# Attention results: added by VectorE one pair of steps later and stored by the loading queue

## The reference, cut to what matters

```
z      = q @ k.T * scale
log_nb = where(key < query, log_sigmoid(-z), 0)
excl   = reverse_cumsum(log_nb) - log_nb
a      = where(key < query, exp(z + log_sigmoid(-z) + excl), 0)
out    = a @ v
```

## Time and profile before

| quantity | value |
|---|---|
| median of 3 runs (lowest, highest) | 4323.52 us (4323.11, 4325.3) |
| time of the profiled execution | 4328.02 us |
| span inside that execution | 4326.2 us |
| TensorE, VectorE, ScalarE busy share of the span | 95%, 63%, 58% |
| attention, from about 1030 to 2330 us | about 1300 us |

### The profile page before, as it was taken

One profiled execution on the slowest core, in us unless ns is written; L12 is line 12 of the kernel. 1 busy time (PEld: TensorE's weight loads), 2 busy tenths in 40 slices (PEclk: granted clock), 3 DMA queues, 4 the chain that ended last, 5 costly groups with the idle time before them and its releaser, 6 DMA issues. The chain is left out here.

```text
span 4326.2 us, 83388 instructions
## 1 busy us (share of the span) xinstructions
PE 4105.9 (95%) x27983; PEld 3104.5 (72%) x27985; DVE 2704.5 (63%) x3882; ACT 2488.0 (58%) x3370; POOL 598.0 (14%) x790
## 2 busy tenths in 40 slices
PE   8999989997999999999998999869999999999997
PEld 6888867774555555555555888758888888888886
DVE  3222235668888888888885555467666655555665
ACT  4222225556887887888885333246665655545665
POOL 0000002231000000000000111102332332323332
PEclk9999999998999999999999999989999999999999
DMA  5444353313112112111103434247666654555674
GB/s 200 182 144 180 146 180 110 124 68 115 31 31 61 31 31 61 31 31 53 36 7 104 147 145 155 106 167 258 226 241 221 227 202 165 204 193 199 242 262 144
DMA packets 308634, 590.36 MB, mean 136 GB/s; under 512 B 38704, under 2 KB 104240, under 8 KB 308400
## 3 DMA queue, kind: packets, MB, share of 16 engines
q1 hardware_dynamic: 257568, 460.82, 30.4%
q0 software_dynamic: 46224, 118.03, 8.0%
q10 hardware_dynamic: 4608, 8.39, 0.5%
HBM read 427.75 MB, written 209.72 MB: 147 GB/s over the span
## 5 line engine op out<-in xcount | busy, mean ns | idle before, releaser
L1115 ACT ACTIVATE att_RT<-att_rt 128x1024 f32<-128x1024 f32 (+1 forms) x576 | 550.5, 956 | 229.5 <-PE att_rt L1053 193.0
L1168 DVE TENSOR_TENSOR_SCAN att_R<-att_stay,att_R 128x257 f32<-128x257 f32 x896 | 625.5, 740 | 62.4 <-ACT att_stay L1105 57.5
L1053 PEld LDWEIGHTS att_rt<-ident,att_R 64*128 64x128 f32 x8448 | 319.3, 139 | 361.6 <-issue 361.4
L1105 ACT ACTIVATE att_stay<-att_z 128x1024 f32<-128x1024 f32 (+2 forms) x576 | 547.5, 951 | 5.9 <-PE att_z L1039 5.9
L1068 PE MATMUL att_out<-att_RT,att_dv 128*64 128x512 f32 (+3 forms) x2304 | 519.8, 572 | 0.0
L1053 PE MATMUL att_rt<-ident,att_R 64*128 64x64 f32 x8448 | 388.8, 229 | 73.3 <-ACT att_RT L1115 65.4
L1594 DVE TENSOR_TENSOR ew_lo<-ew_raw,ew_hi 128x1024 fp32r<-128x1024 f32 x384 | 444.2, 1219 | 21.8 <-ACT ew_hi L1587 13.6
L1587 ACT ACTIVATE ew_hi<-ew_raw 128x1024 fp32r<-128x1024 f32 x384 | 374.1, 1048 | 100.1 <-PE ex_down L1982 93.3
L1171 DVE TENSOR_TENSOR att_R<-att_stay,att_R 128x512 f32<-128x512 f32 x448 | 312.4, 697 | 47.1 <-DVE att_R L1168 0.5
L236 PE MATMUL qkv_out<-u_u_hi,qkv_w_hi 128*128 128x512 f32 x768 | 309.3, 403 | 3.0 <-DVE u_u_lo L227 3.0
L236 PE MATMUL qkv_out<-u_u_hi,qkv_w_lo 128*128 128x512 f32 x768 | 301.1, 392 | 0.0
(11 more groups left out here) (282 smaller groups left out, 8432.4 us busy)
## 6 DMA issues: line engine op xcount, KB each, us to landing
ew_raw<-in_w_e_gate SPq DMA_DIRECT2D x32, 2048.0 KB, 9.1
ew_raw<-in_w_e_up SPq DMA_DIRECT2D x32, 2048.0 KB, 9.9
ew_raw<-in_w_e_down SPq DMA_DIRECT2D x32, 2048.0 KB, 9.1
u_x<-in_x SPq DMA_DIRECT2D x32, 512.0 KB, 5.9
s_u_hi<-u_u_hi SPq DMA_DIRECT2D x8, 2048.0 KB, 11.9
s_u_lo<-u_u_lo SPq DMA_DIRECT2D x8, 2048.0 KB, 16.5
mix_x<-in_x SPq DMA_DIRECT2D x32, 512.0 KB, 4.9
s_h<-mix_h SPq DMA_DIRECT2D x32, 512.0 KB, 3.7
```

Of the source, the lines that this page charges most:

```text
L1053: last = nc.tensor.transpose(rt[:, half, qt, h, :], R[lanes, n % 3, qt, h, s * P:(s + 1) * P], k.ident[lanes, lanes])
L1105: done = nc.scalar.activation(stay[:, step % 4, :, 0:width], z_pair[:, :, 0:width], ACT.Sigmoid, scale=-scale)
L1115: nc.scalar.activation(RT[:, s, first:, :, :, :].rearrange("p t h half q -> p (t h) half q"), turned_pair, ACT.Copy).then_inc(rt_copied, 1)
L1168: nc.vector.tensor_tensor_scan(R[:, n % 3, s, h, 0::2][:, ::-1], kept[:, 1::2][:, ::-1], kept[:, 0::2][:, ::-1], R[:, (n - 1) % 3, s, h, 0 ...
```

## The change

ScalarE's `results` and its store go. VectorE adds the four blocks of 128 columns in one `tensor_tensor`, with `v_last` broadcast along the 128 columns, at the end of the pair of steps after the one in which the group ended; where the group ends with the last pair of steps of a pair of heads, it does so in that same pair. SP issues the stores: inside the loop after the load of the same group's queries for the next pair of heads, and for the last pair of heads after the loads for the next stage, group 7's ahead of them.

```diff
+        def store_results(sp, hp, G):
+            hold(sp, k, out_copied, 2 + hp * NG + (NG - 1 - G) + 1)
+            sp.dma_start(io.mix_t[bass.ds(hp * P, P), G * GT:(G + 1) * GT],
+                         stage[:, bank_of(G), :]).then_inc(stored[bank_of(G)], 16)
+
         @block.sync
         def _(sp):
+            for s in stored:
+                sp.sem_inc(s, 16)
             load_values(sp, 0, NG - 1)
...
                     load_queries(sp, hp, g)
+                    store_results(sp, hp - 1, g)
+            store_results(sp, NP - 1, NG - 1)
             sp.wait_ge(stored[0], 16 * ((NP - 1) * NG // 2 + 2))
             for t in range(2):
                 load_mix(sp, k, io, 0, t)
             for c in range(next_weights.depth):
                 next_weights.load(sp, c)
+            for g in range(NG - 2, -1, -1):
+                store_results(sp, NP - 1, g)
+            for s in stored:
+                sp.wait_ge(s, 16 * (NP * NG // 2 + 1))
...
-        def results(act, hp, step):
-            G, c, s = unit_of(step)
-            if s != 3 or c != 0:
-                return
-            j = NG - 1 - G
-            act.wait_ge(av_done, 4 + hp * K + step + 1)
-            act.wait_ge(stored[bank_of(G)], hp * 16 * (NG // 2) + 16 * (j // 2) + 16)
-            for qt in range(TT):
-                cols = slice(qt * P, (qt + 1) * P)
-                done = nc.scalar.activation(stage[:, bank_of(G), cols], out[bank_of(G)][:, cols], ACT.Identity,
-                                            bias=k.v_last[:, bass.ds(hp * NT + G * TT + qt, 1)])
-            done.then_inc(out_copied, 1)
-            act.wait_ge(out_copied, 2 + hp * NG + j + 1)
-            act.dma_start(io.mix_t[bass.ds(hp * P, P), G * GT:(G + 1) * GT],
-                          stage[:, bank_of(G), :]).then_inc(stored[bank_of(G)], 16)
-
...
-            if i >= 0:
-                results(act, hp, 2 * i + 1)
...
+        def results(dve, hp, step):
+
+            G, c, s = unit_of(step)
+            if s != 3 or c != 0:
+                return
+            j = NG - 1 - G
+            dve.wait_ge(av_done, 4 + hp * K + step + 1)
+            dve.wait_ge(stored[bank_of(G)], hp * 16 * (NG // 2) + 16 * (j // 2) + 16)
+            tiles = lambda ap: ap.rearrange("p (t q) -> p t q", q=P)
+            last_values = k.v_last[:, bass.ds(hp * NT + G * TT, TT)].unsqueeze(2).to_broadcast([P, TT, P])
+            nc.vector.tensor_tensor(tiles(stage[:, bank_of(G), :]), tiles(out[bank_of(G)][:]), last_values,
+                                    ALU.add).then_inc(out_copied, 1)
+
         def dve_pair(dve, hp, i, end):
...
                     scans(dve, hp, step + SCORE_LEAD)
+            if i > 0:
+                results(dve, hp, 2 * i - 1)
+            if i == K // 2 - 1:
+                results(dve, hp, 2 * i + 1)
```

More of the change, by code:

```diff
@@ L1140, in act_pair @@
                     sigmoids(act, hp, 2 * i + SCORE_LEAD + half)
-            if i >= 0:
-                results(act, hp, 2 * i + 1)
         @block.scalar
         def _(act):
-            for s in stored:
-                act.sem_inc(s, 16)
             over_heads(act, act_pair)
-            for s in stored:
-                act.wait_ge(s, 16 * (NP * NG // 2 + 1))
         def scans(dve, hp, step):
```

## The result

| | before | after |
|---|---|---|
| median | 4324.41 us (4 runs) | 4285.6 us (4 runs, 4285.09 to 4286.55) |
| ratio of the two, with its 95% interval | 1 | 0.9908 (0.9897 to 0.992) |
| profiled execution, its span | 4328.02, 4326.2 us | 4285.09, 4283.3 us |

The change gave 38.8 us. I had forecast 27.8, with a range from 4288 to 4310: the direction was right, the size was 11 us short, and the measured time lies outside the range.

A forecast was written before the change was run, and what follows sets the result against it. TensorE was taken to set the pace, with gaps hanging on ScalarE's results at group ends. 29.9 - 1.3 - 2.0 - 0.3 + 1.2 + 0.3 = 27.8 us, off the 4323.5 median: about 4296, range 4288 to 4310.

The forecast's parts named there:

- What bounds the kernel: In the attention TensorE sets the pace, busy 309 of 326 us per pair of heads; time can come only from its gaps.
- part 1: At group ends, ScalarE loses its additions, waits and store issues, so its copy starts earlier; stalls go except 1.3 us kept.
- the term of the sum for these stalls: TensorE's stalls at 28 query-group ends, summed from the timeline: 3 x 7.9 + 6.2 = 29.9 us.
- the term of the passages: Where the loop goes back between pairs of heads, ScalarE's earlier start gains 0.6 us twice: 1.2 us.
- Part 2: VectorE's added 128x512 addition per group end takes 0.65 us, mostly hidden; 2.0 us lost over 21 looped ends.
- The passage to the straight code: Before the last pair of heads VectorE is already late, so TensorE's gains of 0.97 and 1.41 are cut to about 0.7 us.
- Part 3: Stores issued by SP cost 0, as the next load comes later anyway; the last store gains 0.3 us.
- The price by the page: For VectorE's addition reading PSUM, the skill's rule adds 0.065 us, losing about 1.4 us of gain; the forecast followed the trace.
- VectorE dear: VectorE's addition takes about 1.3 us instead of 0.65, losing 13 us at 21 ends: 4309; chance 0.1.
- the stall moves: TensorE meets its next one-buffer wait or hand-overs at group ends, giving half back: 4309; chance 0.15.
- VectorE the bound: Around group ends an addition of 2.2 us makes VectorE the limit, 12 us slower: 4335; chance 0.05.
- The fourth: Stores on SP hold the loads or the barrier at the end as much as was won: 4323; chance 0.05.

The follow-up runs named there:

- same pair: Against the kernel after, VectorE's addition stands at the end of the pair of steps in which the group ended, not one later; 4283.4 us.
- only the store: Against the kernel before, ScalarE keeps its four additions, but the wait for them and the store leave it and SP stores; 4295.1 us.
- ScalarE adds a pair later: Against the kernel before, ScalarE does its four additions one pair of steps later without waiting for them, and SP stores; 4285.2 us.
- eight additions: Against the kernel after, VectorE's one addition of 512 columns per group end becomes eight of 64; 4296.1 us.

## Why the prediction was wrong

**What bounds the kernel, and part 1.** Right. The stalls after the ends were the loss; they went, whole but for the 0.86 us at the last, and with them the 28 waits of ScalarE behind its own results. The step that failed is the term of the sum for these stalls: 29.9 us for 28 ends, less 1.3 kept, so 28.6. From start to start the two traces give 33.5 for the same ends. The second miss is the term of the passages, 1.2 where 4.5 came.

| term of the sum | forecast | measured |
|---|---|---|
| ends of groups 7 to 1, loop, VectorE's cost taken off | 23.7 - 0.3 - 2.0 - 0.3 = 21.1 | 25.8 |
| last pair of heads and the last store | 6.2 - 1.0 + 0.3 = 5.5 | 5.74 + 1.95 = 7.7 |
| the passages | 1.2 | 4.5 |
| sum | 27.8 | 38.0 |

- *Brackets taken for the cost.* I added up the idle time that the rows print. From start to start each stall was 0.15 to 0.2 us longer: 28 of them make the 5 us between 28.6 and 33.5, 3.8 in the first line and 1.1 in the second. The rest of the first line is VectorE's cost, which was smaller. The rest of the second is mainly three steps of 0.28 us away from the ends that went too, and 0.5 us gained between the last products and the next stage, for 0.3 forecast. Why those steps went I don't know.
- *The range.* Its low end was "all the stalls gone", 33 us. That was no bound, since it was made of the same brackets.
- *ScalarE's 0.30 ahead of the additions* I read as a wait for TensorE's last products, after the bracket's releaser. Without the loop the additions start 0.10 us after the sigmoid, so most of it was not that wait; the register instructions in the queue there fit. This did not change the sum, but it hid that the loop had a part in it.

**The passages.** I gave 0.6 us to each jump, between 0 and 0.86, because TensorE's products there had a hole that might take the gain back. There was no hole. The products took 3.25 us because TensorE was at its lower clock, which I had not looked at: the granted clock by stretch was there to be read, and the 0.99 of the earlier trace rows was its trace. In the kernel before:

```profile
1356.00:1360.00 4.00, 3.14 (x14) 1.10 (x14) 1.27 (x2) 2.71 (x4) 0.00 (x0) 0.50 0.01 4
```

0.50 is the lower of the two levels, 1.2 GHz. After the first jump of the kernel after, the products took 2.90 us and after the second 1.73:

```profile
1344.72 2.90 PE L1081 MATMUL att_out<-att_RT,att_dv 128*64 128x512 f32 x8
...
1661.51 1.73 PE L1081 MATMUL att_out<-att_RT,att_dv 128*64 128x512 f32 x8
```

The clock around them:

```profile
1340.00:1344.00 4.00, 2.78 (x20) 2.48 (x22) 3.65 (x6) 1.26 (x2) 0.00 (x0) 0.54 0.22 76
...
1660.00:1664.00 4.00, 4.00 (x44) 2.59 (x42) 1.99 (x4) 2.85 (x4) 0.00 (x0) 1.00 0.01 2
```

In all looped kernels TensorE stood for 2.6 to 3.3 us at each jump. Behind that it was at the lower level for about 6.8 us in both passages of both traces of the kernel before, for 6.8 and 0 us in the kernel after, and for 0 to 6.8 us in the others; with the loop written out the clock stayed at 1.00 in every passage. Four kernels had one passage with 6.8 us and one with none: the slow one took 1.4 us more in the kernel after, 1.8 in "same pair", and 2.6 in "only the store" and "ScalarE adds a pair later". So of the 4.5 us gained in the passages about 1.4 or more hang on the clock, which did not fall in the second one. That part was neither forecast nor a sure effect of the change: in "same pair" it was the first passage that kept the clock. What decides it stays open, since stops of 2.67 and 2.76 us came out differently. With the clock low in both, the first passage gained 1.76 us, still above the bound of 0.86: the next matmuls came earlier by more than the one bracket that I had taken as the limit. What the engines do while they stand at a jump, no run shows; that I called it a refill of instructions was an inference.

**Part 2.** Price right (684 ns for 691), total cost right (2 us for the 2.3 allowed). Its place was off: not a tenth everywhere, but 0.4 us at one unit, (2, 0), and under 0.1 at the others. The rows show it as a wait of 0.34 us for VectorE at 1302.06 in the kernel after. My sign that part 2 is wrong was a new wait of transposes for VectorE of over 5 us. The row has 9.2, but 5.4 of it are the two stops at the jumps (2.67 and 2.76), which stood in the kernel before too, as 3.17 and 2.78; the new waits sum to 3.7, so by that sign part 2 stands.

The passage to the straight code was right: TensorE gained 1.08 us over two ends there, for 0.7 forecast, and waits for VectorE at 1978.76, 1.25 us. That the addition has to stand a pair later for VectorE's sake was wrong.

**Part 3.** Right. SP issues the store at 1105.15 and the next load 0.7 us behind it, 8.27 us after the load before it; in the kernel before it was 8.05. So the load comes 0.2 us later, and no engine's wait in the attention is put down to a load. ScalarE as issuer does as well in the loop, in another place.

**The price by the page.** The Trainium skill, page "Perfetto Trace Analysis", section "Optimizing Scalar/DVE Operations", gives VectorE more overhead on PSUM than on SBUF. In this kernel the row that reads PSUM is 684 ns and the one from SBUF 698: no surcharge is to be seen in the recorded durations, though the two rows differ in their operands too. The advice to keep inputs and outputs on separate issuing engines stands on the same page in the section "DMA Optimizations", not in the one that I named, and only as what may make sense; that a load would come late by it was my own reading. It made no difference at this load: 4285.6 us with the stores on SP, 4284.8 with those of groups 7 to 1 on ScalarE.

**Rivals.** The first three (VectorE dear, the stall moves, VectorE the bound) did not come true. The eight additions show that the first mechanism is real, at 0.27 us of time on average for 0.44 us of work. The fourth (nothing changes, because of SP) did not come true either.

## What to carry to other kernels

Measure a stall on TensorE from the start of one matmul to the start of the next, and compare it with the same distance where nothing waits; the printed idle time was short by 0.15 to 0.2 us here, and a bound made of it is no bound. Where matmuls of one shape take longer than elsewhere, read the granted clock of that stretch before calling the difference a hole. On an engine that others wait for in every step, take out first the wait for its own result: with the store behind it, it was most of the loss, and it is gone whether the work moves to another engine or only one pair of steps on. Where a value in a wait or an address depends on a loop's index, and where engines jump, look at the same code written out before tuning further: here that was worth 10 to 22 us.

## What the runs showed of the hardware that I had not expected

- Register instructions of 43 to 60 ns each stand in ScalarE's queue before the additions in the looped code, and not in the straight code. With the loop written out ScalarE's two gaps at the end of group 7 were 0.43 us shorter together.
- A passage with a jump of all engines took 19.1 to 22.9 us, without one 16.5 to 17.4 (18.7 with eight additions). TensorE stood for 2.6 to 3.3 us at each jump, and the granted clock was at its lower level for 0 to 6.8 us behind it; two passages of one execution differ by up to 2.6 us with that.
- A small addition, 128x64, costs VectorE about 0.14 us in a row of eight (1.14 us for all), so eight cost 1.7 times one of 128x512.
